# Sliding attention of a two-block fp32 kernel: the query scale goes into the rotation tables, tiles are rotated in pairs, and the last two pairs are rotated inside the attention

## The reference, cut to what matters

```
q = rmsnorm(x, g) @ w_q                       # 256 x 1024, 16 heads of 64
q = apply_partial_rope(q, cos, sin)           # on the first 16 of 64 features
s = q k^T / 8, masked to a window of 128 and 16 meta keys
m = max(max(s), sink);  p = exp(s - m);  p = p / (sum(p) + exp(sink - m))
o = p @ v;   x = x + o @ w_out
```

## Time and profile before

| | us |
|---|---|
| median of 3 runs | 1767.87 |
| lowest and highest run | 1767.27, 1770.1 |
| the profiled execution, from first to last instruction | 1768.9 |
| PE busy | 1734.3 (98%) |
| DVE busy | 1057.3 (60%) |
| ACT busy | 724.8 (41%) |

### The profile page before, as it was taken

The page is one execution under the profiler, slowest core; times in us unless marked ns, Lnnn a source line. Parts: engine busy times, 40 slices in busy tenths (PEclk is TensorE's granted clock), DMA queues, the critical chain, the costliest instruction groups (busy, mean ns, idle before and its releaser), DMA issues.

```text
span 1768.9 us, 31465 instructions
## 1 busy us (share of the span) xinstructions
PE 1734.3 (98%) x12356; PEld 1404.7 (79%) x12356; DVE 1057.3 (60%) x1915; ACT 724.8 (41%) x1175; POOL 21.2 (1%) x26
## 2 busy tenths in 40 slices
PE   9999999999999999999999999999999999999997
PEld 8999989899999999997799999998953333333332
DVE  7775566787755877568787756867762222222223
ACT  6444462464444544455654445957521101110110
POOL 0000000100000000000000001000020000000000
PEclk9999999999999999998999999999999999999999
DMA  6555334435553454532245545443789999999996
GB/s 245 185 179 191 128 132 155 73 134 193 184 196 138 143 183 178 208 125 92 96 167 190 210 171 191 144 167 117 303 341 427 427 427 428 429 428 428 427 427 260
DMA packets 42341, 409.71 MB, mean 232 GB/s; under 512 B 5305, under 2 KB 5305, under 8 KB 7057
## 3 DMA queue, kind: packets, MB, share of 16 engines
q1 hardware_dynamic: 40032, 402.21, 58.3%
q0 software_dynamic: 1936, 5.79, 1.6%
q10 hardware_dynamic: 288, 0.52, 0.1%
HBM read 405.87 MB, written 2.63 MB: 231 GB/s over the span
## 4 chain that ended last, share of the span: by engine, by line
PE 86%; DMA 6%; DVE 5%; ACT 2%; issue 1%; SPq 0%; DVEq 0%; ACTq 0%
PE ps L604 84%; PE ps L608 2%; DMA branch<-w_gate_up 2%; DMA late<-w_gate_up 2%; DMA soon<-w_gate_up 1%; DVE w_lo L1783 1%; DMA raw<-w_units 1%; ACT w_hi L1311 1%; DVE branch L1825 0%; ACT arena L1572 0%; DVE x_lo L1846 0%; DVE x_lo L1848 0%; DVE branch L1812 0%; ACT arena L1555 0%; DVE h L1898 0%
## 5 line engine op out<-in xcount | busy, mean ns | idle before, releaser
L604 PE MATMUL ps<-x_hi,w_hi 128*128 128x256 f32 (+1 forms) x2144 | 614.7, 287 | 3.0 <-DVE x_lo L1846 1.8
L604 PE MATMUL ps<-x_lo,w_hi 128*128 128x256 f32 (+1 forms) x2144 | 610.4, 285 | 0.0
L604 PE MATMUL ps<-x_hi,w_lo 128*128 128x256 f32 (+1 forms) x2144 | 608.8, 284 | 0.0
L1783 DVE TENSOR_TENSOR w_lo<-raw,w_hi 128x1024 fp32r<-128x1024 f32 (+1 forms) x352 | 448.1, 1293 | 136.1 <-ACT w_hi L1311 135.6
L1311 ACT ACTIVATE w_hi<-raw 128x1024 fp32r<-128x1024 f32 (+1 forms) x352 | 385.3, 1114 | 203.0 <-PE ps L604 130.5
L604 PEld LDWEIGHTS ps<-x_hi,w_hi 128*128 128x128 f32 x2144 | 403.6, 188 | 9.2 <-issue 5.1
L604 PEld LDWEIGHTS ps<-x_hi,w_lo 128*128 128x128 f32 x2144 | 405.6, 189 | 0.0
L604 PEld LDWEIGHTS ps<-x_lo,w_hi 128*128 128x128 f32 x2144 | 404.6, 189 | 0.3
L604 PE MATMUL ps<-hid_hi,w_hi 128*128 128x272 f32 (+1 forms) x720 | 206.0, 286 | 0.8 <-DVE hid_lo L1848 0.4
L604 PE MATMUL ps<-hid_hi,w_lo 128*128 128x272 f32 (+1 forms) x720 | 204.6, 284 | 0.0
L604 PE MATMUL ps<-hid_lo,w_hi 128*128 128x272 f32 (+1 forms) x720 | 204.0, 283 | 0.0
(11 more groups left out here) (337 smaller groups left out, 1996.9 us busy)
## 6 DMA issues: line engine op xcount, KB each, us to landing
raw<-w_units SPq DMA_DIRECT2D x144, 1024.0 KB, 4.8
soon<-w_gate_up SPq DMA_DIRECT2D x32, 2048.0 KB, 22.0
late<-w_gate_up SPq DMA_DIRECT2D x24, 2048.0 KB, 21.2
raw<-w_out_units SPq DMA_DIRECT2D x32, 1408.0 KB, 6.1
soon<-w_down SPq DMA_DIRECT2D x16, 2048.0 KB, 24.9
late<-w_down SPq DMA_DIRECT2D x12, 2048.0 KB, 22.3
branch<-w_gate_up SPq DMA_DIRECT2D x8, 2048.0 KB, 22.9
branch<-w_down SPq DMA_DIRECT2D x4, 2048.0 KB, 20.5
```

What stands on the lines that cost most here:

```text
L604: return nc.tensor.matmul(out_ap, lhsT, rhs, start=start, stop=stop, skip_group_check=True)
L1783: v.tensor_tensor(part(w_lo, c, 0, n), raw_slot(u, j * n, n), part(w_hi, c, 0, n).bitcast(F32), ALU.subtract).then_inc(lo_made, 1)
```

## The change

- `rs` is multiplied once into a table of cosines and sines (`s_turn`, 512 columns, one DVE instruction). The eight scalings of query tiles on DVE are gone. Tiles 4 to 7 are copied out of PSUM by ACT instead, as tiles 0 to 3 already were.
- DVE rotates a pair of tiles with three instructions of 512 columns; PE puts a pair's two matmuls into one bank. `qrot` has 4 uses of banks 4 and 5 instead of 8.
- PE: pair 0 is rotated behind unit 1, pair 1 within unit 2, and `scores(0)` stands within unit 3. Then come the matmuls of pair 2, `scores(1)`, the matmuls of pair 3 and the router's constants, which now use bank 7.
- DVE: pairs 0 and 1 are rotated ahead of `maxima(0)`, pair 2 between `maxima(1)` and `normalise(0)`, pair 3 behind `normalise(1)`, after the router's constants. The split of the unit `sout + 0` moves from ahead of the rotations to behind `normalise(2)`.
- ACT: the split of `sout + 1`'s first half moves from ahead of the attention to behind the exponentials of group 1.

```diff
@@ plan
-        tiles("qrot", [4, 5], 8)
-        tiles("rconst", [6], 1)
+        tiles("qrot", [4, 5], 4)
+        tiles("rconst", [7], 1)
@@ tensor
             def rotate(j):
+                t = plan["qrot"].at(j)
+                bank = free(t)
+                for n in range(2):
+                    i = 2 * j + n
+                    taken(plan["sq"][1].at(i))
+                    m = mm(bank[:, n * SEQ:(n + 1) * SEQ], C("rot"), s_q[:, i * SEQ:(i + 1) * SEQ], True, True)
+                m.then_inc(full[t[0]], 1)
+            project(u0, T, 0, X, SEQ, x_base=48, made=3)
+            project(u0 + 1, T, 2, X, SEQ, between=lambda: stat(8, SEQ), begun=1)
+            rotate(0)
+            project(u0 + 2, T, 4, X, SEQ, between=lambda: rotate(1))
...
+            def last_queries(scores):
+                project(u0 + 3, T, 6, X, SEQ, between=lambda: scores(0))
+                rotate(2)
+                scores(1)
+                rotate(3)
+                router_constants()
...
-                   SWA_KEYS, SWA_TURNS, lambda g: pe.wait_ge(q_roped, g + 1), router_constants)
+                   SWA_KEYS, SWA_TURNS, lambda g: pe.wait_ge(q_roped, g // 2 + 1), opening=last_queries)
@@ scalar
-            split_to(plan["sout"][0] + 1, 1)
+            split_to(plan["sq"][0] + 3)
+            for i in range(RAW_TILES, 8):
+                if i == 6:
+                    split_to(plan["sout"][0])
+                t = plan["sq"][1].at(i)
+                nc.scalar.activation(s_q[:, i * SEQ:(i + 1) * SEQ], filled(t)[:, 0:SEQ], ACT.Copy).then_inc(evac[t[0]], 1)
...
                     if g + 1 < groups:
                         exponents(g + 1)
+                    if g == 0 and sinks:
+                        split_to(plan["sout"][0] + 1, 1)
@@ vector
+            then(v.tensor_tensor(s_turn..., cst[cos, sin]..., rs[:, 0:SEQ]..., ALU.mult))
+            def rotate(j):
+                t = plan["qrot"].at(j)
+                bank = filled(t)
+                q, x = two_tiles(s_q[:, 2 * j * SEQ:2 * (j + 1) * SEQ]), two_tiles(s_t[j % 2])
+                did(v.tensor_tensor(q, q, turn_table(0), ALU.mult))
+                v.tensor_tensor(x, two_tiles(bank[:, :]), turn_table(1), ALU.mult).then_inc(evac[t[0]], 1)
+                own()
+                mine(t)
                 v.tensor_tensor(q, q, x, ALU.add).then_inc(q_roped, 1)
+            split_to(plan["sq"][0] + 3)
+            then(v.tensor_scalar(small[:, NEG_SINK:NEG_SINK + 32], W("sinks"), -1.0, None, ALU.mult))
+            rotate(0)
+            rotate(1)
...
+            def after_group(g):
+                if g == 0:
+                    router_constants()
+                    rotate(3)
+                elif g == 1:
+                    split_to(plan["sout"][0])
+                elif g == 3:
+                    split_to(plan["sout"][0] + 1, 1)
             attend(("ss",), 8, 0, a_p, P + META, SWA_ROW, lambda g, b: (C("swa0"), C("swa1")), True,
-                   lambda g: split_to(plan["sout"][0] + 1, 1) if g == 3 else None, router_constants)
+                   after_group, lambda g: rotate(2) if g == 1 else None)
```

More of the change, by code:

```diff
@@ L244, in two_blocks @@
         s_q = room(KT * SEQ)
-        s_t = room(2 * SEQ)
+        s_t = [room(2 * SEQ) for _ in range(2)]
+        s_turn = room(2 * SEQ)
         s_o = room(KT * SEQ)
@@ L882, in rotate @@
             def rotate(j):
[L883 to L897, removed]
+                t = plan["qrot"].at(j)
[9 more added lines that the diff above has]
+            project(u0 + 2, T, 4, X, SEQ, between=lambda: rotate(1))
             def attend(names, groups, first, pbs, pTs, second, row, q_of, k_of, v_of, places, turns, done, values=None,
-                       ahead=2, between=None):
+                       ahead=2, between=None, opening=None):
                 S, TT, V = (plan[x] for x in names)
@@ L944, in outputs @@
                     m.then_inc(full[t[0]], 1)
-                scores(0)
-                scores(1)
-                if values is not None:
+                if opening is not None:
+                    opening(scores)
+                else:
+                    scores(0)
+                    scores(1)
                     values()
@@ L2150, in _, with two_tiles, turn_table @@
             inverse_rms(8, SEQ)
-            def rotate(i):
-                t = plan["qrot"].at(i)
-                bank = filled(t)
[L2156 to L2163, removed]
+            at = C_COLS["cos"][0]
+            own()
+            then(v.tensor_tensor(s_turn.rearrange("p (a t) -> p a t", a=2),
+                                 cst[:, at:at + 2 * TA].rearrange("p (a t) -> p a t", a=2)[:, :, 0:SEQ],
+                                 rs[:, 0:SEQ].rearrange("p (a t) -> p a t", a=1).to_broadcast([P, 2, SEQ]), ALU.mult))
+            def two_tiles(x):
+                return x.rearrange("p (a t) -> p a t", a=2)
+            def turn_table(n):
+                return s_turn[:, n * SEQ:(n + 1) * SEQ].rearrange("p (a t) -> p a t", a=1).to_broadcast([P, 2, SEQ])
+            def rotate(j):
+                t = plan["qrot"].at(j)
+                bank = filled(t)
+                q, x = two_tiles(s_q[:, 2 * j * SEQ:2 * (j + 1) * SEQ]), two_tiles(s_t[j % 2])
+                did(v.tensor_tensor(q, q, turn_table(0), ALU.mult))
+                v.tensor_tensor(x, two_tiles(bank[:, :]), turn_table(1), ALU.mult).then_inc(evac[t[0]], 1)
                 own()
@@ L2245, in attend, with router_constants @@
                         between(g)
[L2247 to L2255 removed]
+            def router_constants():
+                t = plan["rconst"].at(0)
+                bank = filled(t)
+                did(v.tensor_scalar(small[:, R_SUM], bank[:, 0:36], -1.0, None, ALU.mult))
+                v.tensor_tensor(small[:, R_BIAS], bank[:, 64:100], W("b_route"), ALU.add).then_inc(evac[t[0]], 1)
+            def after_group(g):
[6 more added lines that the diff above has]
+                    split_to(plan["sout"][0] + 1, 1)
             attend(("ss",), 8, 0, a_p, P + META, SWA_ROW, lambda g, b: (C("swa0"), C("swa1")), True,
[L2257 removed]
+                   after_group, lambda g: rotate(2) if g == 1 else None)
             for m in range(KT):
```

23 lines of the change are left out of this document (2 added, 21 removed).

## The result

The changed kernel takes 1771.36 us (median; 1770.5 to 1772.57), the kernel before 1767.47 us in the same runs (1765.53 to 1770.1). The ratio is 1.0022, 95% interval 1.0014 to 1.0029. It is slower by 3.9 us, where 0.9 us less was predicted, and it lies above the predicted range, which ended at 1770.8. One execution of after_pad, a kernel further down, took 3405.34 us and is left out of its ratio; over its other eleven the median is 1770.18 us.

What follows compares the result with a forecast made beforehand. PE was taken to bound the kernel, busy 98%, with DVE bounding the opening. Of 4.3 us won, the wait for pair 3 left 2.1 and the low clock 0.9: 1767.87 to 1767.0 us, range 1764 to 1770.8.

Steps and rivals of the forecast that it cites:

- PE's opening without a gap: From 798 to about 818.6 PE would run without a gap, `scores(2)` starting at 818.6 instead of 822.96.
- pair 3's sine product: In `turns_of(0)`, PE would wait 4.1 us for bank 5 until DVE's sine product of pair 3, at 824.1.
- No scores waited for pair 0: Rival, chance 0.05: scores within unit 3 wait for pair 0, giving 1767.9; the prediction saw 2.5 us of cover.
- The runs before have their median 1.0 lower: Starting point: from the profiled execution's 1768.9 us to the runs' median of 1767.87.
- of the 4.3 us ahead: At the end of `turns_of(0)`: of 4.3 us won by the earlier `scores(2)`, 2.1 are left after the wait.
- 843.7 + 1.2: Last exponentials: 843.7 at full clock instead of 845.84, then later by the low clock's 1.4 us less 0.2.
- The clock's term: Behind the standstill, low clock for 6 transposes, `scores(3)` and a bit of `turns_of(1)` makes `maxima(3)` 1.4 us later.
- Of this DVE catches up little, some 0.2: After `maxima(3)`, DVE recovers some 0.2 of the 1.4 us lost to low clock, leaving a gain of 0.9.
- the pace of the later groups: Behind the split, DVE takes 2.97 us a group, and 4.58 us for `maxima(6)`, `normalise(5)` and `maxima(7)`.
- what is won ahead reaches the end undiminished: Ahead of the expert-weight stage: an earlier start shifts that stage as a whole, so the gain stays whole.
- slower: the clock stays low: Rival, chance 0.15: early attention groups stay at low clock, 3.0 us a group; 1768.7 to 1770, or 1772.
- DVE has 2 x 1.98 and 2.27 us extra against 0.55 spare: Early attention groups: two pair rotations and the split on DVE exceed its spare time per group, so PE stands still.

Runs made afterwards that it cites:

- after_pad: The changed kernel with 30 waits on DVE and 4 on PE that are met at once; 1770.28 us, ratio 1.0014.
- again: The changed kernel run once more without an edit; 1770.54 us, ratio 1.0023.
- pair3_first: The changed kernel with DVE rotating pair 3 right behind `normalise(0)`, banks unchanged; 1769.59 us, ratio 1.0009.
- before_b: Another profiled execution of the kernel before, without an edit; span 1766.7 us.
- bank7_split: bank7 with DVE's split of `sout + 0` moved behind `maxima(0)`; 1768.03 us, ratio 0.9995.
- after: The changed kernel itself, in its first set of runs; 1771.36 us, ratio 1.0022.
- fill: The changed kernel with 11 idle matmuls that nobody reads while PE waits for pair 3; 1771.9 us, ratio 1.0028.
- bank7: The changed kernel with pair 3's product in bank 7 and the router's constants in bank 6, read first by DVE; 1769.33 us, ratio 1.0010.
- bank7_split_pad: bank7_split with the added waits of after_pad; 1766.35 us, ratio 0.9993.

## Why the prediction was wrong, step by step

**Right:** PE's opening without a gap; pair 3's sine product as the one that holds PE, in the middle of `turns_of(0)`; 3.97 us of standstill for 4.1; 0.68 and 0.69 us for the 512-column instructions; a low clock behind it. The last is partly luck: it was expected because of the standstill, and in again the clock was low ahead of the standstill, in pair3_first without one. The end of the attention's chain to the projection was read as 7.77 us and is 7.76. No scores waited for pair 0.

**The starting point, 1.6 us.** "The runs before have their median 1.0 lower" compares a median of times with a span. Times lie 2.0 us above spans here, so the execution read was some 3 us above the median. It had 1.6 us of this surplus in the changed part itself (55.97 against 54.4). The step that failed with it is "of the 4.3 us ahead": `scores(2)` comes 23.99 - 21.49 = 2.5 us earlier than in an ordinary execution of before, not 4.3. Against before_b, `scores(3)` is then already 28.50 - 28.01 = 0.5 us late when the standstill is over. Had 2.5 been put where 4.3 stood, the same working would have given a loss.

**The end of the attention, 1.5 us.** The prediction had 843.7 + 1.2 for the last exponentials, 844.0 when shifted by the 0.92 us of this execution; they began at 845.54. 0.5 of that was there at the end of the standstill (823.2 reckoned, 823.75 measured): the opening had been taken 0.8 too short, 0.6 of it in pairs 2 and 3, whose matmuls took 0.95 and 0.97 us from start to start and not 0.67, and the router 0.3 too long (3.59 us for 3.9). The clock's term was right in size where it counts. From the resumption to `maxima(3)` there are 827.01 - 823.75 = 3.26 us, and 0.75 + 0.90 at full clock, 1.6 us of loss where 1.4 had been put. That the clock then stays low for `turns_of(1)` and `outputs(0)`, 1.5 us more of PE's time, costs nothing further, because DVE is behind by then. What failed is "Of this DVE catches up little, some 0.2" and the pace of the later groups (10.41 us from `maxima(4)` to `maxima(7)` instead of 10.1, and 2.87 instead of 2.5 us from there to the exponentials).

How far DVE had become the bound is seen beside the kernel before. There, DVE still waited for PE's scores in each of these groups (before_b, first instructions of `maxima(3)` to `maxima(5)`):

```profile
826.73 0.37 DVE L2200 CUSTOM_DVE_ANT_0 arena<-ps,cst,small 128x144 f32<-128x144 f32 x1 [0.77 <-PE ps L604]
...
830.25 0.37 DVE L2200 CUSTOM_DVE_ANT_0 arena<-ps,cst,small 128x144 f32<-128x144 f32 x1 [0.46 <-PE ps L604]
...
833.78 0.37 DVE L2200 CUSTOM_DVE_ANT_0 arena<-ps,cst,small 128x144 f32<-128x144 f32 x1 [0.45 <-PE ps L604]
```

In the changed kernel DVE idles only 0.25 us between 827.01 and `maxima(7)`, so that 827.01 to 842.67 is 15.66 us where PE's pace would give four times 3.53. The difference of 1.5 us is the split of `sout + 0`, which before lay ahead of the attention. bank7_split has shown it as 1.8.

**The last projection, 0.6 to 0.8 us.** No term stood for it. The prediction took it that what is won ahead reaches the end undiminished. For the first 216.41 us from the output projection on, the same in before_b and the changed kernel, that is so, but the code behind the change also lies at other addresses. Nothing in the trace of before says what this would do.

**Between the two projections, a gain of 0 to 1.4 us.** No term stood for this either. From the start of the output projection to the stretch of the last one, before_b and then the changed kernel:

```profile
851.51:1259.55 408.04, 400.49 (x3308) 393.42 (x3307) 294.05 (x465) 239.29 (x367) 5.33 (x10) 0.99 0.47 169
```

```profile
853.30:1260.01 406.71, 399.19 (x3309) 391.95 (x3308) 293.21 (x464) 239.20 (x367) 5.33 (x10) 1.00 0.47 169
```

The difference is one stretch of 3.5 to 4 us at the low clock, 224 us behind the output projection's start. Three of the four executions of before have it (408.04 to 408.11 us), the fourth (406.74) and the changed kernel's two (406.71, 406.72) don't. Both executions with the added waits have it; of the eight of rebuilt kernels without them two do. What decides it wasn't settled.

**The routing behind it, 0 to 1.5 us, open.** In the 36 us behind that stretch the granted clock is 0.95 in all four executions of before and 0.91 in the changed kernel's first. The expert weights arrive at 307 instead of 323 GB/s there; at the 427 GB/s of the stage that follows, 36 x 16 / 427 = 1.3 us of loading are missing. It is 0.91 in four of the eight profiled executions of unpadded rebuilt kernels (after, fill, bank7, pair3_first), 0.95 in three and 1.00 in one, and 0.95 in both padded ones. Whether the code's place does that or the moment at which the clock falls wasn't settled.

**The sum.** 2.1 to 2.7 us in the attention, 0.6 to 0.8 in the last projection and 0 to 1.5 behind it, less 0 to 1.4 between the projections, make 1.3 to 5.0. That holds the 3.9 and the 3.0 us by which the medians differ in the two sets of runs, and is too wide to prove them. Laid against before_b alone, the span of the changed kernel's first execution is 2.8 us longer: 0.4 less ahead of `stat(8)`, then +2.2, -1.3, +0.8 and +1.5. That of its second is 1.0 us longer: 0.9 less, then +2.6, -1.3, +0.6 and 0.0. So the profiled executions place 1.0 to 2.8 us; the rest of the medians' difference stays open, although bank7_split, which differs from the changed kernel in the attention alone, is level with the kernel before. Of the rivals, *slower: the clock stays low* named the right sign and 1768.7 to 1770, by a mechanism that turned out not to be the price: the clock was low long, but its second half lay beside DVE's chain. The cause stood in the same paragraph, as a reason for it: "DVE has 2 x 1.98 and 2.27 us extra against 0.55 spare". That, with the standstill, makes the loss in the attention.

## What to carry to other kernels

A trace is one execution: before a gain of 1 us is reckoned from a stage of 56 us, the same stage should be seen in several executions, and a span is never set against a median of times. Where work is moved behind other work, list the bank that its operand occupies and who fills that bank next. Work that must lie inside a stage goes where the trace shows its engine idle: the same split cost 1.8 us less in a gap of 3.11 us than in the chain of the groups.

## What the runs showed of the hardware

- The same kernel, in four executions, had the granted clock at its lower level (1.2 GHz) in different places, and the same part took 54.35 to 55.97 us. The Trainium skill, in TensorE: Matmul & The Clock Gate, What's actually happening, calls the number of matmuls made at the low clock when a kernel starts run-variable. These executions show the same in the middle of a kernel.
- A PE standstill of 3.97 us behind the router's matmuls was followed by a clock of 0.50 for 5.5 us. With idle matmuls in it (fill), or without it (bank7, bank7_split, bank7_split_pad), the clock stayed at 1.00 in one execution each. But in again it was 0.50 ahead of the standstill, and in pair3_first it was 0.50 for nearly 6.8 us without one.
- Thirty-four waits that are met at once, 450 us ahead, took 0.5 to 0.8 us off a stretch of the last projection (30.38 and 30.11 to 29.59 us), and a fetch of instructions no longer fell into a weight load there.
